# A hybrid decoder layer in split fp32: the first hidden group of both FFNs becomes six plain up steps, with the activation blocks combined beside them

## The chip, the cores and the metric

The kernel runs on one NeuronCore of a Trainium2 chip. The time is device microseconds of one launch, the median of three runs. The profile is one execution, recorded by the hardware profiler; all its times count from the start of its span.

## The reference, cut to what matters

One layer of a decoder over 544 tokens (512 of a prompt, 32 of samples), held as columns: activations are 128 partitions x 8 tiles x 544 tokens, the tokens in two halves of 272. Four sub-layers follow one another; the change touches the first and the third.

```python
def swiglu(h, w_in, w_out):
    gu = h @ w_in
    g, u = jnp.split(gu, 2, axis=-1)
    return (jax.nn.silu(g) * u) @ w_out

x = x + 0.5 * rmsnorm(swiglu(rmsnorm(x, f1_pre), f1_in, f1_out), f1_post)     # f1
...                                                                            # mixer
x = x + 0.5 * rmsnorm(swiglu(rmsnorm(x, f2_pre), f2_in, f2_out), f2_post)     # f2
...                                                                            # gated embedding
```

D_MODEL is 1024 (KD = 8 tiles of 128), D_FF is 2816 (F_TILES = 22 tiles of 128).

## The kernel before, in words

**Split fp32.** Every dense product is done as three fp32r products: each operand is split into a high part (a ScalarE copy, `w_hi`, `a_hi`, `h_hi`) and the rest (a VectorE subtraction, `w_lo`, `a_lo`, `h_lo`), and TensorE runs hi x hi, hi x lo, lo x hi. So each weight tile goes HBM -> `raw` (two slots, queue of SyncE) -> ScalarE -> VectorE -> TensorE. The load of weight w waits until weight w-2 is split.

**Groups.** An FFN runs over the 22 hidden tiles in groups, `GROUPS = (8, 8, 6)`: the up steps of a group (`f1_up0`), then its down products (`f1_down0`), then the next group. An up step makes one hidden tile: gate and up product, norm factor (`out_of`, L1911 and L1912), silu on ScalarE, product, split (`h_hi`, `h_lo`). Down products are 8 (KD) per group; each reads all hidden tiles of the group, 6 matmuls of 272 columns per tile, so 48 with 8 hidden tiles and 36 with 6. Partial sums of the groups are added in `y`.

**Plain and mixed steps.** The first `PLAIN` = 4 up steps of an FFN are plain (`dense`, L570): 8 k-tiles x gate and up x 3 x 2 halves = 96 matmuls. The other 18 are mixed (`up_mixed`, L765): a Strassen-like scheme over 2 x 2 blocks (k-tiles 0 to 3 and 4 to 7, by token halves) with 7 block products instead of 8, so 84 matmuls. It needs combined activation blocks: the normed values (`block_values`, L1990), two differences (L2001, L2003), two sums (L2009, L2012), and the split of seven blocks (`block_high` L1400, `block_low` L1996). Combined weights are made in `mix_front`. In the kernel before all this block work is put among the plain steps, and the last blocks lie in `a_hi`, `a_lo`, which the last plain step must have read (`a_gone`).

**Order.** Each engine has one instruction stream written by hand. On ScalarE and VectorE a weight split stands in it between the other work; an engine whose next instruction waits holds all behind it. The plain steps of f2 begin in halves (`edge_first`, `edge_second`): steps 0 to 2 of f2 are computed before the norm factor of the second half is known.

**End of an FFN.** The last group's down products 4 to 7 stand beside the first weight splits of the next stage, in the order that `edge_splits` gives:

```python
return {4: [(last, 5), (last, 6)], 5: [(last, 7), after[0]], 6: [after[1]], 7: after[2:]}
```

The splits at key 4 wait until down product 3 is done. The squares of each finished `y` tile are summed on GpSimd (L2623), and TensorE sums them over partitions (L604) in the middle of the last down product.

Of the kernel before, what the change touches and what calls it, by code (L numbers as in the profile page):

```python
# [13 lines left out]
F32 = mybir.dt.float32  # L14
# [6 lines left out]
P = 128  # L21
# [16 lines left out]
GROUPS = (8, 8, 6)  # L38
G_FIRST = (0, 8, 16)
G_MAX = max(GROUPS)  # L40
PLAIN = 4
# [74 lines left out]
def build(nc, a, o):  # L116
# [13 lines left out]
    with ctx:  # L130
# [122 lines left out]
        b_part = {11: y[:, 0:4, 0, :], 12: y[:, 0:4, 1, :], 21: y[:, 4:8, 0, :], 22: y[:, 4:8, 1, :]}  # L253
# [60 lines left out]
        def before(m):  # L314
# [31 lines left out]
        sum_quad = {0: (T0["f1_up0"] + 1) % 2, 1: (T0["f1_down2"] + KD - 1) % 2, 2: T0["in"] % 2,  # L346
                    3: T0["f2_up0"] % 2, 4: T0["f2_up0"] % 2, 5: (T0["f2_down2"] + KD - 1) % 2, 6: T0["gate"] % 2,
                    7: T0["end"] % 2}
        EDGES = {0: "in", 1: "f2_up0", 2: "gate"}
        LAST = {0: ("f1_down2", KD - 1), 1: ("out", 3), 2: ("f2_down2", KD - 1), 3: ("gate", 3)}  # L350
# [11 lines left out]
        for name in ("f1_down2", "f2_down2"):  # L362
            for n in range(3):
                PLACED[W0[name] + 5 + n] = tuple(t_[:, 1280 * n:1280 * (n + 1)] for t_ in a_flat)
# [3 lines left out]
        PLACED[W0["f2_up0"] + 2] = tuple(t_[:, 4 * T:4 * T + SLOT] for t_ in h_flat)  # L368
# [178 lines left out]
        def _(pe):  # L547
# [202 lines left out]
            def up_mixed(name, first, n):  # L750
# [34 lines left out]
                if first:  # L785
                    body(Step(first), 7 * (f == "f2"))
                    first += 1
                steps(pe, first, n, body)

            def ffn(name, b, first):  # L790
                up_mixed(f"{name}_up0", PLAIN, GROUPS[0])
                product(f"{name}_down0", KD, 1, GROUPS[0], H, h_tiles(first))
                up_mixed(f"{name}_up1", 0, GROUPS[1])
                product(f"{name}_down1", KD, 1, GROUPS[1], H, h_tiles(first + G_FIRST[1]))
                up_mixed(f"{name}_up2", 0, GROUPS[2])
                product(f"{name}_down2", KD, 1, GROUPS[2], H, h_tiles(first + G_FIRST[2]), loop=5, end=KD - 1)
                edge_last(b, H, GROUPS[2], 1)
# [423 lines left out]
            edge_second(1)  # L1221
            plain_end("f2")
# [12 lines left out]
        def _(act):  # L1235
# [161 lines left out]
            def block_high(f, n):  # L1397

                act.wait_ge(*((sig["b_made"], 8 * f + 8) if n < 2 else (sig["t_made"], 4 * f + 4)))
                fn(B_PAIR[n][0], B_RAW[n], ACT.Copy).then_inc(sig["t_hi"], 1)  # L1400

            def plain_end(name):


                f, up0, st, first = int(name == "f2"), f"{name}_up0", Step(PLAIN - 1), Step(PLAIN)
                act.wait_ge(sig["psum_full"], ticket(st, up0)[0])
                mix_front(up0, first)
# [3 lines left out]
                mix_begin(up0, first)  # L1411
                block_high(f, 6)
                snap(up0, first, 0)
                up_gate(up0, st)
                mix_high(up0, first, 1)
                up_high(up0, st)

            def up_mixed(name, first, n):


                def body(st, last=False, begun=False):
                    if not begun:
                        snap(name, st, 0)
# [16 lines left out]
                if first:  # L1440
                    body(Step(first), begun=True)
                    first += 1
                else:
                    mix_high(name, Step(0), 1)
                steps(act, first, n - 1, body)
                body(Step(n - 1), last=True)

            def down0(st, t, quad, use):
# [15 lines left out]
            def ffn(name, b, after):  # L1464

                j = 2 * b + 1
                up_mixed(f"{name}_up0", PLAIN, GROUPS[0])
                stage(f"{name}_down0", KD, down0, follow=f"{name}_up1")
                up_mixed(f"{name}_up1", 0, GROUPS[1])
                stage(f"{name}_down1", KD, lambda st, t, quad, use: None, follow=f"{name}_up2")  # L1470
                up_mixed(f"{name}_up2", 0, GROUPS[2])
                nc.scalar.preload_act_table_set("natural_log_exp_and_others")
                last = f"{name}_down2"
# [32 lines left out]
            stage("f1_up0", GROUPS[0], up("f1_up0"), first=1, end=2)  # L1506
            for n in range(2):
                block_high(0, n)
            stage("f1_up0", GROUPS[0], up("f1_up0"), first=2, end=3)
            block_high(0, 2)  # L1510
            plain_end("f1")
# [227 lines left out]
            norm(4, 1)  # L1739
            split_edge("f2_up0", 3, T0["f2_up0"] + 2)  # L1740
            nc.scalar.preload_act_table(ACT.Silu)
            for c in range(3):
                up("f2_up0")(Step(c), *ticket(Step(c), "f2_up0"))
                for n in ((), (0, 1), (2,))[c]:
                    block_high(1, n)
# [9 lines left out]
            def between(half, k):  # L1755
                if half == 0 and k in (1, 3):
                    e_tiles(k // 2)
                if half == 0 and k == 4:
                    split_edge("gate", 1, T0["f2_down2"] + KD)
                    e_tiles(2)  # L1760
                    e_tiles(3)
# [30 lines left out]
        def _(dve):  # L1792
# [158 lines left out]
            def up_mixed(name, first, n):  # L1951
# [26 lines left out]
                if first:  # L1978
                    body(Step(first))
# [833 lines left out]
```

## Time and profile before

| | |
|---|---|
| median of 3 runs (1239.47 to 1240.24) | 1239.5 us |
| the profiled execution, own time | 1242.34 us |
| its span | 1240.6 us |
| TensorE matmul busy | 1167.4 us (94%) |
| VectorE / ScalarE / GpSimd busy | 801.5 / 565.5 / 98.7 us |
| mean granted TensorE clock | 0.974 |

How to read it: matmuls follow one another closer than a single one lasts (290 ns on average, every 126 ns), so the pace is read from a stretch with its count. TensorE is busy nearly throughout, and its idle stretches are few; which work ends each of them is what counts.

### The profile page before, as it was taken

To read this page: it belongs to the slowest core of one execution; us is meant where nothing else is said; L and a number is where in the kernel's file an instruction comes from. 1 tells how busy PE (TensorE), PEld (TensorE's weight loads), DVE (VectorE), ACT (ScalarE), POOL (GpSimd) and SP (SyncE) were. 2 spreads that over 40 slices of the span, in tenths; PEclk is the share of its full clock that TensorE was granted. 3 is DMA by queue.
4 is the path that set the end of the run, shared out by engine and by line. 5 is a ranking of instruction groups with operands and counts; after the bars stand their busy time and mean duration, and the time that the engine had idled before them with its cause. 6 is when DMAs were issued, how large, how long until landed. Compare 5 with 4: busy or idle time off the path is not lost.

```text
span 1240.6 us, 22901 instructions
## 1 busy us (share of the span) xinstructions
PE 1167.4 (94%) x9150; PEld 1125.3 (91%) x9150; DVE 801.5 (65%) x1103; ACT 565.5 (46%) x776; POOL 98.7 (8%) x139
## 2 busy tenths in 40 slices
PE   7789999999998799999998999879999999999895
PEld 7789999999998789999877699879999999999894
DVE  5796278736854756555378747697268835864666
ACT  5364245523543432311389745355245522553544
POOL 1500000000002002112040010000000000002002
PEclk9899999999999799999998999989999999999997
DMA  5222332224213122113055251122243223314202
GB/s 209 69 68 69 102 121 92 73 88 132 84 52 124 35 69 85 61 63 107 1 167 193 69 170 35 35 72 66 85 136 101 68 86 118 102 39 134 99 1 73
DMA packets 45420, 110.26 MB, mean 89 GB/s; under 512 B 5474, under 2 KB 11634, under 8 KB 45218
## 3 DMA queue, kind: packets, MB, share of 16 engines
q1 hardware_dynamic: 43538, 103.13, 25.4%
q0 software_dynamic: 1232, 5.01, 1.2%
q8 instruction: 52, 0.85, 0.3%
q10 hardware_dynamic: 576, 1.08, 0.2%
q14 instruction: 22, 0.18, 0.0%
HBM read 103.57 MB, written 5.64 MB: 88 GB/s over the span
## 4 chain that ended last, share of the span: by engine, by line
PE 82%; DVE 9%; ACT 5%; issue 2%; DMA 1%; SPq 0%; POOL 0%; DVEq 0%; ACTq 0%
PE PS L570 34%; PE PS L765 29%; PE PS L583 9%; PE PS L880 1%; PE PS L1056 1%; DVE w_lo L1800 1%; PE PS L735 1%; ACT w_hi L1243 1%; PE PS L604 1%; DVE y L1990 1%; PE PS L907 1%; DVE a_lo L1996 1%; DMA raw<-in_ple_w_up 0%; PE PS L937 0%; PE PS L981 0%
## 5 line engine op out<-in xcount | busy, mean ns | idle before, releaser
L1800 DVE TENSOR_TENSOR w_lo<-raw,w_hi 128x1024 fp32r<-128x1024 f32 (+2 forms) x74 | 104.1, 1407 | 111.1 <-ACT w_hi L1243 111.1
L765 PE MATMUL PS<-a_hi,w_hi 128*128 128x272 f32 x576 | 167.0, 290 | 3.4 <-issue 3.4
L765 PE MATMUL PS<-a_lo,w_hi 128*128 128x272 f32 x576 | 167.7, 291 | 0.0
L765 PE MATMUL PS<-a_hi,w_lo 128*128 128x272 f32 x576 | 166.9, 290 | 0.0
L1243 ACT ACTIVATE w_hi<-raw 128x1024 fp32r<-128x1024 f32 (+2 forms) x75 | 88.9, 1185 | 143.1 <-PE PS L570 120.5
L570 PE MATMUL PS<-h_hi,w_hi 128*128 128x272 f32 x632 | 130.9, 288 | 2.0 <-DVE w_lo L1800 2.0
L570 PE MATMUL PS<-a_hi,w_hi 128*128 128x272 f32 x528 | 115.4, 301 | 18.4 <-DVE w_lo L2099 7.1
L570 PE MATMUL PS<-h_hi,w_lo 128*128 128x272 f32 x632 | 130.9, 289 | 0.0
L570 PE MATMUL PS<-h_lo,w_hi 128*128 128x272 f32 x632 | 130.4, 288 | 0.0
L765 PEld LDWEIGHTS PS<-a_hi,w_hi 128*128 128x128 f32 x576 | 109.3, 190 | 4.0 <-issue 3.8
L570 PE MATMUL PS<-a_lo,w_hi 128*128 128x272 f32 x528 | 112.2, 295 | 0.0
L570 PE MATMUL PS<-a_hi,w_lo 128*128 128x272 f32 x528 | 111.8, 294 | 0.0
L765 PE MATMUL PS<-b_tail,w_hi 128*128 128x272 f32 x576 | 110.6, 290 | 0.0
L765 PEld LDWEIGHTS PS<-a_hi,w_lo 128*128 128x128 f32 x576 | 109.2, 190 | 0.0
L765 PEld LDWEIGHTS PS<-a_lo,w_hi 128*128 128x128 f32 x576 | 108.9, 189 | 0.0
L570 PEld LDWEIGHTS PS<-a_hi,w_hi 128*128 128x128 f32 x528 | 86.1, 196 | 22.9 <-issue 13.4
L570 PEld LDWEIGHTS PS<-h_hi,w_hi 128*128 128x128 f32 x632 | 99.4, 188 | 2.4 <-issue 2.4
L570 PEld LDWEIGHTS PS<-h_lo,w_hi 128*128 128x128 f32 x632 | 99.4, 189 | 0.0
L570 PEld LDWEIGHTS PS<-h_hi,w_lo 128*128 128x128 f32 x632 | 98.7, 189 | 0.0
L765 PEld LDWEIGHTS PS<-b_tail,w_hi 128*128 128x128 f32 x576 | 90.8, 189 | 0.0
L570 PEld LDWEIGHTS PS<-a_lo,w_hi 128*128 128x128 f32 x528 | 86.3, 196 | 0.0
L570 PEld LDWEIGHTS PS<-a_hi,w_lo 128*128 128x128 f32 x528 | 85.6, 195 | 0.0
(468 smaller groups left out, 2636.6 us busy)
## 6 DMA issues: line engine op xcount, KB each, us to landing
raw<-in_f_in SPq DMA_DIRECT2D x86, 512.0 KB, 4.3
raw<-in_f_out SPq DMA_DIRECT2D x64, 256.0 KB, 2.8
raw<-in_w_rest SPq DMA_DIRECT2D x40, 256.0 KB, 2.9
raw<-in_f_out SPq DMA_DIRECT2D x32, 192.0 KB, 2.4
raw<-in_w_out SPq DMA_DIRECT2D x8, 512.0 KB, 4.4
raw<-in_ple_w_gate SPq DMA_DIRECT2D x8, 512.0 KB, 4.5
x<-in_x SPq DMA_DIRECT2D x8, 272.0 KB, 6.8
out<-x SPq DMA_DIRECT2D x8, 272.0 KB, 2.2
```

The costliest lines, as they stand in the source:

```text
L570: last = mm(PS[0:width, 4 * quad + 2 * c + half, 0:HALF], wt[:, cols], act[:, k, half * HALF:(half + 1) * HALF], start=(k == 0 and n == 0) ...
L583: last = mm(PS[0:width, 4 * quad + 2 * c + half, 0:HALF], wt[:, cols], act[:, k, tok], start=(k == 0 and n == 0), stop=(k == n_k - 1 and n ...
L604: last = mm(PS[:, 4 * quad + 2 + half, 0:HALF], ones[:], squares[:, tok], start=(k < summed), stop=(k == KD - 1))
L735: last = mm(PS[:, 4 * (t % 2) + 2 * c + half, 0:HALF], wt[:, slot, col:col + P], act[:, k, half * HALF:(half + 1) * HALF], start=(k == 0 a ...
L765: last = mm(PS[:, 4 * quad + bank, 0:HALF], w_[:, k * P:(k + 1) * P], a_[:, k, :], start=(start and k == 0 and i == 0), stop=(stop and k = ...
L880: last = mm(PS[:, 2 + hh, tok], k_[r, tok], q_[r, tok], start=True, stop=True)
L907: last = mm(PS[:, 7, n * 256:n * 256 + 256], kl_batch[:, 2 * part + n, :], gv_new[:, p * 256:(p + 1) * 256], start=True, stop=True)
L1056: last = mm(out, mask, src, start=start and i == 0, stop=stop and i == 1)
L1243: fn(pair[0][:, 0:width], raw[:, slot, 0:width], ACT.Copy).then_inc(sig["split_hi"], 1)
L1800: v.tensor_tensor(pair[1][:, 0:width], raw[:, slot, 0:width], pair[0][:, 0:width].bitcast(F32), ALU.subtract).then_inc(sig["split_lo"], 1)
L1990: v.scalar_tensor_tensor(flat(y[:, k]), flat(x[:, k]), vec[:, c:c + 1], flat(rstd[:, 0]), ALU.mult, ALU.mult).then_inc(sig["b_made"], 1)
L1996: v.tensor_tensor(B_PAIR[n][1], B_RAW[n], B_PAIR[n][0].bitcast(F32), ALU.subtract).then_inc(sig["t_lo"], 1)
```

## The change

- `GROUPS` is (6, 8, 8), and `PLAIN` is the first group: all six up steps of it are plain, its down products (36 matmuls each) come next, and only then the 16 mixed steps.
- The raw blocks of the second token half are written into the slots of hidden tiles 6 and 7, which the first group does not use. `block_values` makes half tiles (16 instructions of 272 columns instead of 8 of 544), some at a time; differences and sums are single instructions between the parts of the plain steps.
- `plain_end` splits the weights of the first two down products, and the last four blocks beside them.

```diff
-GROUPS = (8, 8, 6)
-G_FIRST = (0, 8, 16)
+GROUPS = (6, 8, 8)
+G_FIRST = (0, 6, 14)
-PLAIN = 4
+ENDS = len(GROUPS) - 1
+PLAIN = GROUPS[0]
...
-        b_part = {11: y[:, 0:4, 0, :], 12: y[:, 0:4, 1, :], 21: y[:, 4:8, 0, :], 22: y[:, 4:8, 1, :]}
+        h_end = [scratch(hold_h[:], (n * G_MAX - 2) * T, [P, 4, HALF]) for n in (1, 2)]
+        b_part = {11: y[:, 0:4, 0, :], 12: h_end[0], 21: y[:, 4:8, 0, :], 22: h_end[1]}
...
             def plain_end(name):        # ScalarE
-                act.wait_ge(sig["psum_full"], ticket(st, up0)[0])
-                mix_front(up0, first)
+                split(st, up0, ticket(st, up0)[0])
                 for n in range(3, 6):
                     act.wait_ge(sig["a_gone"], 3 * f + n - 2)
                     block_high(f, n)
-                mix_begin(up0, first)
+                split(Step(0), down0, ticket(Step(0), down0)[0])
+                up_gate(up0, st)
                 block_high(f, 6)
...
-            def block_values(f):
-                for k in range(KD):
+            def block_values(f, half, first, end):
+                for k in range(first, end):
                     c = VEC[f"f{f + 1}_pre"] + k
-                    v.scalar_tensor_tensor(flat(y[:, k]), flat(x[:, k]), vec[:, c:c + 1], flat(rstd[:, 0]), ALU.mult,
+                    v.scalar_tensor_tensor(b_part[10 * (k // 4 + 1) + half + 1][:, k % 4, :], x[:, k, half, :],
+                                           vec[:, c:c + 1], rstd[:, 0, half, :], ALU.mult,
                                            ALU.mult).then_inc(sig["b_made"], 1)
...
             def plain_end(name, j):     # VectorE
+                split(st, up0)
+                block_low(f, 3)
+                block_low(f, 4)
                 out_of(up0, j, st, t, quad, use)
+                split(Step(0), f"{name}_down0")
+                product_of(up0, st, quad, use)
+                block_low(f, 5)
+                up_low(up0, st)
                 block_low(f, 6)
...
-            up("f1_up0", 0)(Step(0), *ticket(Step(0), "f1_up0"))
-            block_values(0)
-            stage("f1_up0", GROUPS[0], up("f1_up0", 0), first=1, end=2)
+            out_of("f1_up0", 0, st, t, quad, use)
+            block_values(0, 0, 0, 1)
+            product_of("f1_up0", st, quad, use)
+            block_values(0, 0, 1, 3)
+            up_low("f1_up0", st)
+            block_values(0, 0, 3, 4)
+            st = Step(1)
+            split(st, "f1_up0")
+            block_values(0, 0, 4, 8)
+            block_values(0, 1, 0, 2)
...
```

**VectorE at the start of f1.** The rows follow the sum of squares; `work<-PS,rstd` is `out_of`, `w_lo<-raw,w_hi 128x2048` the split of the weights of plain step 2. Before:

```order
L1911 TENSOR_TENSOR work<-PS,rstd 128x544
L1912 TENSOR_TENSOR work<-PS,rstd 128x544
L1902 TENSOR_TENSOR work<-work 128x544
L1917 TENSOR_TENSOR h_lo<-work,h_hi 128x544
L1990 SCALAR_TENSOR_TENSOR y<-x,vec,rstd 128x544 x8
L1800 TENSOR_TENSOR w_lo<-raw,w_hi 128x2048
```

VectorE at the same place in the changed kernel:

```order
L1913 TENSOR_TENSOR work<-PS,rstd 128x544
L1914 TENSOR_TENSOR work<-PS,rstd 128x544
L1988 SCALAR_TENSOR_TENSOR y<-x,vec,rstd 128x272
L2020 TENSOR_TENSOR work<-work 128x544
L1988 SCALAR_TENSOR_TENSOR y<-x,vec,rstd 128x272 x2
L1919 TENSOR_TENSOR h_lo<-work,h_hi 128x544
L1988 SCALAR_TENSOR_TENSOR y<-x,vec,rstd 128x272
L1804 TENSOR_TENSOR w_lo<-raw,w_hi 128x2048
L1988 SCALAR_TENSOR_TENSOR y<-x,vec,rstd 128x272 x4
L1988 SCALAR_TENSOR_TENSOR hold_h<-x,vec,rstd 128x272 x2
```

Four half tiles of values stand ahead of the split now instead of eight whole ones.

**VectorE in f2, from the weights of step 3 to those of step 4, in the changed kernel** (`b_extra`, `b_tail` are split blocks, `y<-y,hold_h` and `hold_h<-hold_h` differences, `extra<-` and `y<-extra,y` sums):

```order
L1804 TENSOR_TENSOR w_lo<-raw,w_hi 128x2048
L2020 TENSOR_TENSOR work<-work 128x544
...
L2002 TENSOR_TENSOR y<-y,hold_h 128x4x272
L1988 SCALAR_TENSOR_TENSOR hold_h<-x,vec,rstd 128x272 x4
L1913 TENSOR_TENSOR work<-PS,rstd 128x544
L1914 TENSOR_TENSOR work<-PS,rstd 128x544
L1995 TENSOR_TENSOR b_tail<-y,b_tail 128x1088
L2020 TENSOR_TENSOR work<-work 128x544
L2005 TENSOR_TENSOR hold_h<-hold_h 128x1088
L1919 TENSOR_TENSOR h_lo<-work,h_hi 128x544
L2012 SCALAR_TENSOR_TENSOR extra<-y,hold_h 128x1088
L2015 SCALAR_TENSOR_TENSOR y<-extra,y 128x4x272
L1804 TENSOR_TENSOR w_lo<-raw,w_hi 128x2048
```

On ScalarE the block copy that needs the last sum stands ahead of the same weights' high part:

```order
L1402 ACTIVATE b_tail<-y 128x1088
L1245 ACTIVATE w_hi<-raw 128x2048
```

In the kernel before there was no plain weight to split after the sums: step 3 was the last plain step, and the mixed weights came next.

**ScalarE beside down products 4 to 7 of the last group of f1.** Before:

```order
L1460 ACTIVATE sq<-y 128x544
L1243 ACTIVATE a_hi<-raw 128x768 x2
L1460 ACTIVATE sq<-y 128x544
L1243 ACTIVATE a_hi<-raw 128x768
L1243 ACTIVATE w_hi<-raw 128x2048
L1460 ACTIVATE sq<-y 128x544
```

The same place in the changed kernel:

```order
L1456 ACTIVATE sq<-y 128x544
L1245 ACTIVATE a_hi<-raw 128x1024 x2
L1456 ACTIVATE sq<-y 128x544
L1245 ACTIVATE a_hi<-raw 128x1024
L1245 ACTIVATE w_hi<-raw 128x2048
L1456 ACTIVATE sq<-y 128x544
```

The order is the same; the down weights are 1024 columns instead of 768, since the last group has 8 hidden tiles.

## Rows read from the trace of the kernel before

**Rows 1.** The page, busy time, share of the span and instructions of each engine

```profile
PE 1167.4 (94%) x9150; PEld 1125.3 (91%) x9150; DVE 801.5 (65%) x1103; ACT 565.5 (46%) x776; POOL 98.7 (8%) x139
```

**Rows 2.** TensorE timeline, plain to mixed steps: start, us, instruction, idle before it

```profile
42.20 0.82 PE L570 MATMUL PS<-a_hi,w_hi 128*128 128x272 f32 x2 [6.42 <-DVE w_lo L1800]
...
69.20 0.52 PE L765 MATMUL PS<-b_extra,w_hi 128*128 128x272 f32 x2 [0.94 <-DVE w_lo L1939]
...
79.66 0.36 PE L765 MATMUL PS<-a_hi,w_hi 128*128 128x272 f32 x1 [2.43 <-issue]
...
800.22 0.70 PE L570 MATMUL PS<-a_hi,w_hi 128*128 128x272 f32 x2 [3.73 <-DVE work L1912]
...
820.57 0.82 PE L765 MATMUL PS<-b_extra,w_hi 128*128 128x272 f32 x2 [6.54 <-DVE w_lo L1939]
```

**Rows 3.** TensorE by stretch: us, PE busy (matmuls), clock, DMA share, GB/s

```profile
42.20:56.00 13.80, 13.80 (x96) 0.86 0.33 102
79.66:84.00 4.34, 4.34 (x22) 0.61 0.02 4
```

**Rows 4.** The chain that ended last: start us, us, what

```profile
116.21 48.11 PE PS L570 x384
164.32 84.74 PE PS L765 x672
...
366.22 13.81 PE PS L570 x108
...
407.34 1.29 PE PS L604 x2
...
1116.44 13.81 PE PS L570 x108
...
1154.08 1.19 PE PS L604 x4
```

**Rows 5.** VectorE timeline, start of f1

```profile
30.16 0.72 DVE L1911 TENSOR_TENSOR work<-PS,rstd 128x544 f32<-128x544 f32 x1 [3.12 <-ACT rstd L1276]
...
34.30 5.65 DVE L1990 SCALAR_TENSOR_TENSOR y<-x,vec,rstd 128x544 f32<-128x544 f32 x8
39.86 2.29 DVE L1800 TENSOR_TENSOR w_lo<-raw,w_hi 128x2048 fp32r<-128x2048 f32 x1
...
48.49 1.30 DVE L2001 TENSOR_TENSOR y<-y 128x1088 f32<-128x1088 f32 x1
```

**Rows 6.** ScalarE timeline, start of f1

```profile
33.53 1.90 ACT L1243 ACTIVATE w_hi<-raw 128x2048 fp32r<-128x2048 f32 x1
...
45.90 1.11 ACT L1400 ACTIVATE b_tail<-y 128x1088 fp32r<-128x1088 f32 x1
```

**Rows 7.** VectorE timeline, edge into f2

```profile
771.86 0.50 DVE L1832 SCALAR_TENSOR_TENSOR a_lo<-x,vec,a_hi 128x272 fp32r<-128x272 f32 x1
772.27 0.50 DVE L1820 SCALAR_TENSOR_TENSOR work<-y,vec,rstd 128x272 f32<-128x272 f32 x1
...
787.06 0.79 DVE L2492 TENSOR_TENSOR work<-PS,rstd 128x272 f32<-128x272 f32 x2 [4.90 <-ACT rstd L1276]
```

**Rows 8.** TensorE timeline, last down products of f1

```profile
366.22 0.51 PE L570 MATMUL PS<-h_hi,w_hi 128*128 128x272 f32 x2 [0.99 <-DVE w_lo L1800]
...
395.76 0.36 PE L583 MATMUL PS<-h_hi,a_hi 128*128 128x272 f32 x1 [2.22 <-DVE y L2034]
...
403.22 0.73 PE L604 MATMUL PS<-sum_sq,ones 128*128 128x272 f32 x2 [3.09 <-POOL sum_sq L2623]
```

**Rows 9.** VectorE and GpSimd timelines, weight splits of down products

```profile
111.28 1.23 DVE L1800 TENSOR_TENSOR w_lo<-raw,w_hi 128x1024 fp32r<-128x1024 f32 x1 [2.12 <-ACT w_hi L1243]
...
368.17 0.96 DVE L1800 TENSOR_TENSOR w_lo<-raw,w_hi 128x768 fp32r<-128x768 f32 x1 [1.46 <-ACT w_hi L1243]
...
372.52 1.36 POOL L2623 TENSOR_TENSOR sum_sq<-sum_sq,sq 128x544 f32<-128x544 f32 x1 [4.42 <-ACT sq L1460]
...
373.21 1.49 DVE L1800 TENSOR_TENSOR w_lo<-raw,w_hi 128x768 fp32r<-128x768 f32 x1 [1.46 <-ACT w_hi L1243]
```

More of the change, by code:

```diff
@@ L783, in body @@
                     part(7, 6, 0, False, True).then_inc(sig["psum_full"], 1)
[L785 to L788, printed above, removed]
+                if begin:
+                    body(Step(0), 7 * (f == "f2"))
+                steps(pe, int(begin), n, body)
             def ffn(name, b, first):
[L791 to L797, printed above, removed]
+                product(f"{name}_down0", KD, 1, PLAIN, H, h_tiles(first))
+                for n in range(1, ENDS + 1):
+                    up_mixed(f"{name}_up{n}", GROUPS[n], n == 1)
+                    last = dict(loop=5, end=KD - 1) if n == ENDS else {}
+                    product(f"{name}_down{n}", KD, 1, GROUPS[n], H, h_tiles(first + G_FIRST[n]), **last)
+                edge_last(b, H, GROUPS[ENDS], 1)
             pe.wait_ge(sig["masks_made"], 1)
@@ L1221, in _ @@
             edge_second(1)
+            product("f2_up0", PLAIN - 1, 2, KD, A, first=3)
             plain_end("f2")
@@ L1466, in ffn @@
                 j = 2 * b + 1
[L1467 to L1471, printed above, removed]
+                stage(f"{name}_down0", KD, down_first, first=1, follow=f"{name}_up1")
+                for n in range(1, ENDS):
+                    up_mixed(f"{name}_up{n}", GROUPS[n])
+                    stage(f"{name}_down{n}", KD, lambda st, t, quad, use: None, follow=f"{name}_up{n + 1}")
+                up_mixed(f"{name}_up{ENDS}", GROUPS[ENDS])
                 nc.scalar.preload_act_table_set("natural_log_exp_and_others")
-                last = f"{name}_down2"
+                last = f"{name}_down{ENDS}"
                 stage(last, KD, down1(j), end=1)
@@ L1505, in _ @@
             up("f1_up0")(Step(0), *ticket(Step(0), "f1_up0"))
[L1506 to L1509, printed above, removed]
+            st = Step(1)
+            split(st, "f1_up0", ticket(st, "f1_up0")[0])
+            block_high(0, 0)
+            up("f1_up0")(st, *ticket(st, "f1_up0"))
+            st = Step(2)
+            split(st, "f1_up0", ticket(st, "f1_up0")[0])
+            block_high(0, 1)
+            up("f1_up0")(st, *ticket(st, "f1_up0"))
             block_high(0, 2)
+            stage("f1_up0", PLAIN, up("f1_up0"), first=3, end=PLAIN - 1)
             plain_end("f1")
@@ L1739, in _ @@
             norm(4, 1)
+            nc.scalar.preload_act_table(ACT.Silu)
+            up("f2_up0")(Step(0), *ticket(Step(0), "f2_up0"))
             split_edge("f2_up0", 3, T0["f2_up0"] + 2)
[L1741 to L1745, printed above, removed]
+            block_high(1, 0)
+            up("f2_up0")(Step(1), *ticket(Step(1), "f2_up0"))
+            block_high(1, 1)
+            up("f2_up0")(Step(2), *ticket(Step(2), "f2_up0"))
+            block_high(1, 2)
+            stage("f2_up0", PLAIN, up("f2_up0"), first=3, end=PLAIN - 1)
             plain_end("f2")
@@ L2005, in block_sums @@
[L2005 to L2012 removed]
+                dve.wait_ge(sig["b_made"], 16 * f + 12 + 4 * n)
```

172 lines of the change are left out of this document (93 added, 79 removed).

## The prediction, before the run

> **What bounds the kernel now.** I read the page first: TensorE is busy 94% of the span [rows 1], so a change pays only by fewer or faster matmuls, or by less of the remaining idle time. The chain of waits says how fast: eight down products of eight hidden tiles are 384 matmuls in 48.11 us, 0.1253 us each, and eight mixed steps are 672 in 84.74 us, 0.1261 each [rows 4]. So a plain step costs 96 x 0.1253 = 12.03 us, a mixed one 10.59, a down product 6.01 us over eight hidden tiles and 4.51 over six. Then I looked in TensorE's timeline for each start with idle time before it. In f1 they are 6.42, 0.94 and 2.43 us, in f2 3.73 and 6.54 [rows 2], all among the first steps. The releaser is mostly VectorE: a weight's low part that stands behind block work in its stream. After two of the long ones the clock is at 1.2 instead of 2.4 GHz for some us: 96 matmuls took 13.80 us (1.8 too many), 22 took 4.34 (1.6 too many) [rows 3]. The last place is the end of an FFN: 0.99, 2.22 and 3.09 us of idle time among the last down products [rows 8].
>
> **The added matmuls.** Two more steps per FFN are plain: 2 x (96 - 84) = 24 matmuls, 24 x 0.1253 = 3.0 us each FFN, +6.0 in all. That is on the path and certain. What comes back must be read from the waits. I do it by placing TensorE in time, from the last point that the change leaves alone to the start of the fifth down product of the last group (I call it s4), which is three products of 4.51 behind the second one: 366.22 + 13.5 = 379.75 in f1, 1116.44 + 13.5 = 1129.97 in f2 [rows 4].
>
> **Start of f1.** TensorE ends step 1 at 42.20 - 6.42 = 35.78 [rows 2]. VectorE begins at 30.16 [rows 5]. Before, all values (5.65 us) stood ahead of the weights of step 2, whose low part began at 39.86. Now four half tiles do. Their price is not in the trace; the nearest row is an operation of the same kind, two tensors and a column scale on 272 columns, 0.50 us, the next one starting 0.41 later [rows 7]. The bounds: 5.65/16 = 0.35 if only columns counted, 0.50 if nothing overlapped. I take 0.41. Four of them fit ahead of 35.4, where ScalarE has made the high part (33.53 + 1.90) [rows 6], so the split runs 35.45 to 37.74 (2.29) [rows 5], and step 2 starts at 37.8: a wait of 2.0 instead of 6.42.
> The Trainium skill (VectorE: DVE Perf Modes, on the TRN2 errata) speaks against the cut into halves: SBUF operations pay a fixed cost per instruction, so small tiles pay it more often. By its cycle table a half tile would be an estimated 0.34 us; the eight in f2's chain below would take 0.6 us less than by my 0.41, and the sum would be 1214.4. The row decides here.
> Does the clock fall after a wait of 2.0? It did after 2.43 and 6.42; after 0.94 the next matmuls kept their pace. I take no fall, and +1.8 as the bound; about 0.6 of that would only eat the next wait.
> From 37.65 VectorE has: six half values 2.5, `out_of` 1.3, a block's low part 1.2, product 0.65, two values 0.8, `h_lo` 0.65, a difference 1.2: the weights of step 3 are split by 48.2, needed at 37.8 + 12.03 = 49.8. Free. Then four values and a low part to 51.0, `out_of` 1.3, difference 1.2, product 0.65 and sum 1.2 with the waits between them, `h_lo` 0.65, the second sum 1.3 (a 1088-column operation lasts 1.30 [rows 5]): 57.2. ScalarE copies that sum, 1.1 us, and only then makes the high part of step 4's weights, 1.9 [rows 6], VectorE the low part, 2.3: 62.45, where step 3 ends at 61.85. Wait 0.6. Steps 4 and 5 end at 62.45 + 24.05 = 86.5; no split stands behind more than an `out_of` there.
> The first down product reads hidden tile 5 last, 30 matmuls in, at 90.3. That tile needs `out_of` 1.4, the split of the second down weights 0.9, product 0.65, one block's low part 1.25, `h_lo` 0.7: 91.4. Wait 1.1.
>
> **Rest of f1.** Eight down products of 4.51, eight mixed steps, eight down products of 6.01, eight mixed steps, four down products of 6.01: 86.5 + 1.1 + 36.1 + 84.7 + 48.1 + 84.7 + 24.05 = 365.3. Before: 379.75. So s4 comes 14.5 us earlier. Of it, +3.0 are matmuls, -10 the waits and slow clock at the start. The other -7 are this: eight products of the first group are 1.5 us shorter each (-12.0), while ahead of s4 only four of the last group are longer (+6.0), and the 0.99 us there goes: the second weights come 5.2 us after the first product's start, which now lasts 6.01.
> In the first group the short products must leave room for the next mixed weights. Those are two ScalarE and VectorE splits of 3.3 us together behind the start of the last down product, 4.51 long: hidden, with 1 us to spare, and +1 per FFN if not.
>
> **Start of f2.** Steps 0 to 2 are unchanged; step 2 ends at 800.22 - 3.73 = 796.5 [rows 2]. VectorE used to wait 4.90 us until 787.06 [rows 7]; eight half values (3.3) lie in it now. After 787.85 come three half values, product and `h_lo` of step 0, `out_of` of step 1 by 792.6: bank free, so the 3.73 goes. Weights of step 3 are split by 794.8, before 796.5. Then, behind them: product, value, `h_lo` to 796.9; low part, difference, four values to 800.9; `out_of`, low part, product, difference, `h_lo`, two sums to 808.45; then ScalarE's copy and high part and VectorE's low part, 1.1 + 1.9 + 2.3: 813.75. Step 3 ends at 808.5. So **a new wait of 5.2 us** stands before step 4 of f2, with the clock down behind it (+1.8, as after 6.42). Step 5 ends at 813.75 + 13.85 + 12.05 = 839.7. The same 1.1 as in f1, then 36.1 + 84.7 + 48.1 + 84.7 + 24.05: s4 at 1118.4, before 1129.97: 11.5 us earlier.
>
> **Behind s4.** Here TensorE is not the bound. The chain runs from the splits that wait for s4 over the loads of the next stage's weights, their splits and the eviction of down product 6 that stands behind them, to the sums at 407.34 and 1154.08 [rows 4]. It hangs on s4, not on how long the products last: TensorE itself would reach its half-way sum at s4 + 4 x 6.01 - 1.1 = 22.95, against 27.6 and 24.1 now. So the longer products 4 to 7 fill the waits of 2.22 and 3.09 and cost nothing. What lengthens the chain is the width of the splits ahead of the first load: 1.23 against 0.96 us for 1024 and 768 columns [rows 9], on both engines, and the next split after it; where GpSimd adds at the same time VectorE's took 1.49 instead of 0.96, so I add the same 0.53 to the wide one. Together +0.75 per FFN, between 0.3 and 1.5.
>
> **Sum.** -14.5 - 11.5 + 1.5 = -24.5 us. The profiled execution took 1242.34 against a span of 1240.6; the 1.7 around it do not change, and I take the difference from the median of the runs, 2.8 below that execution: 1239.5 - 24.5 = 1215.0.
>
> **Rivals.**
> *The end of an FFN stretches with its products* (12%). If the chain behind s4 hangs on later products after all (a load that waits for the split of the seventh weight, an eviction in the queue), products 4 to 7 cost their 6 us in each FFN: 1227. For it: each split at a key of `edge_splits` waits for its own product. Against it: TensorE waits 5.3 us there now.
> *The start gains less* (10%). Low parts and `h_lo` miss their slots, and step 5 and the first down product wait like step 4 of f2: two more waits of 3 to 4 us with some slow clock per FFN, or the whole start gain lost (10 and 7.5 us): 1223 to 1232.
> *The end gains more* (8%). The in-order chain in f2 is 2 us shorter than I count and the clock stays up: 1210.
> *Slower* (3%). Each of plain steps 2 to 5 gets its weights as late as step 2 did before, 6.4 us and 1.8 of slow clock: eight times 8.2 against the 9.6 that I count for all waits of both starts, +56: 1271. It decides from 4.3 us on average per step, where the 24.5 are used up. Only one place, f2's step 4, reaches that by my count.
> *The clock.* The Trainium skill (TensorE: Matmul & The Clock Gate, "What's actually happening") says that the check of activity runs freely and does not start anew with the kernel, so that the same wait can be followed by a fall in one run and not in another. By that page step 4 of f2 might keep its pace, 1213.2, and step 2 of f1 might not, 1216.2. The rows show both kinds only for different waits.
>
> **The numbers.** Likeliest 67%: 1215.0, with 1211 to 1219 from the bounds (half values at 0.35 or 0.50: 1 us either way in f2; the clock -1.8 or +1.2; behind s4 -0.9 or +1.5). The range reaches to the second and third case: 1209 to 1225. A measurement of this kernel tells 0.2%, 2.5 us, from no change. Faster 0.94, within 0.2% 0.02, slower 0.04 (1% of it for what I have not seen).
>
> **What would show it.** In the changed kernel's profile: step 2 of f1 starts near 37.8; idle time of 0 to 1 us before step 4 of f1 and about 5 before step 4 of f2, released by VectorE's weight split; about 1 us inside the first down product of both; the last group of f1 reaches s4 near 365; the waits of 0.99 and 2.22 are gone and that of 3.09 is under 1.5; the half-way sum comes 28 us after s4 in f1. It is wrong if f2's wait is over 8 us, if the first mixed step waits for weights, or if the stretch behind s4 is longer than before by more than 2 us.

## The result, and the profile after

| | before | after |
|---|---|---|
| median of the runs on the same chip | 1239.87 us (1239.47 to 1242.61, 4 runs) | 1217.64 us (1217.07 to 1218.09, 4 runs) |
| ratio, 95% interval | | 0.9818 [0.9804, 0.9833] |
| span of the profiled execution | 1240.6 us | 1216.0 us |
| mean granted TensorE clock | 0.974 | 0.985 |

The change takes 22.2 us off; forecast were 24.5, a time of 1215.0. The two spans differ by 24.6, but 2.4 of that belong to the execution of before that was profiled: from the block of 108 matmuls at the end of f1 to the block of 264 ahead of f2, where no line was changed, it took 290.7 us, while the changed kernel and those of experiments 1 and 2 took 288.2 to 288.3. I leave these 2.4 out below.

The page of after, busy time by engine (before: [rows 1]):

```profile
PE 1163.2 (96%) x9198; PEld 1122.2 (92%) x9198; DVE 784.5 (65%) x1095; ACT 554.2 (46%) x756; POOL 97.5 (8%) x139
```

48 matmuls more, and yet TensorE is busy 4.2 us less: the slow clock of [rows 3] is gone from f1 (some of the 4.2 are slow clock in the 2.4 above). Of TensorE's timeline after, the starts that stand behind idle time (before: [rows 2] and [rows 8]):

```profile
38.02 0.52 PE L573 MATMUL PS<-a_hi,w_hi 128*128 128x272 f32 x2 [2.04 <-DVE w_lo L1804]
62.82 0.52 PE L573 MATMUL PS<-a_hi,w_hi 128*128 128x272 f32 x2 [0.43 <-DVE w_lo L1804]
91.97 0.52 PE L573 MATMUL PS<-h_hi,w_hi 128*128 128x272 f32 x2 [1.03 <-DVE h_lo L1919]
...
385.09 0.36 PE L586 MATMUL PS<-h_hi,a_hi 128*128 128x272 f32 x1 [0.69 <-DVE y L2040]
392.56 0.72 PE L607 MATMUL PS<-sum_sq,ones 128*128 128x272 f32 x2 [2.33 <-POOL sum_sq L2660]
396.61 1.28 PE L607 MATMUL PS<-sq,ones 128*128 128x272 f32 x2 [3.33 <-ACT sq L1300]
...
799.86 0.82 PE L573 MATMUL PS<-a_hi,w_hi 128*128 128x272 f32 x2 [5.34 <-DVE w_lo L1804]
831.17 0.52 PE L573 MATMUL PS<-h_hi,w_hi 128*128 128x272 f32 x2 [1.03 <-DVE h_lo L1919]
```

Step 2 of f1 waits 2.04 instead of 6.42, the mixed steps no longer wait for weights, and the 3.73 of f2 is gone, and f2 has its new wait of 5.34 before step 4. At the end of f1 the 0.99 is gone and the 2.22 has become 0.69. The chain that ended last, after (before: [rows 4]):

```profile
124.48 84.76 PE PS L768 x672
209.25 48.10 PE PS L573 x384
...
342.09 24.30 PE PS L573 x192
...
372.00 7.99 DMA raw<-in_w_in
380.07 1.93 ACT w_hi L1245
...
396.61 1.29 PE PS L607 x2
401.79 4.86 PE PS L586 x24
406.65 0.92 PE PS L607 x4
407.56 13.57 PE PS L586 x108
...
799.86 26.54 PE PS L573 x192
...
1081.29 42.34 PE PS L573 x336
...
1135.39 10.55 PE PS L738 x84
```

The last group now reaches s4 at 342.09 + 4 x 6.01 = 366.1 in f1 (379.75 before) and at 1105.3 in f2. VectorE behind step 2 of f2's plain steps, the place of the new wait (columns: start, us, work, idle before it):

```profile
791.93 1.28 DVE L2012 SCALAR_TENSOR_TENSOR extra<-y,hold_h 128x1088 f32<-128x1088 f32 x1
793.25 1.29 DVE L2015 SCALAR_TENSOR_TENSOR y<-extra,y 128x1088 f32<-128x1088 f32 x1
797.52 2.29 DVE L1804 TENSOR_TENSOR w_lo<-raw,w_hi 128x2048 fp32r<-128x2048 f32 x1 [2.98 <-ACT w_hi L1245]
```

The split stands behind both sums and stands still for 2.98 us more, since ScalarE copies the second sum and only then makes the high part.

### The profile page after: what moved, and what is told of

Read it like the earlier page. It is cut to its first block, busy times and chain, and to the rows that moved or that the text cites. A ratio compares the mean times of both kernels' runs of the same rounds, so it can differ in the third digit from the quotient of the medians.

```text
span 1216.0 us, 23032 instructions
## 1 busy us (share of the span) xinstructions
PE 1163.2 (96%) x9198; PEld 1122.2 (92%) x9198; DVE 784.5 (65%) x1095; ACT 554.2 (46%) x756; POOL 97.5 (8%) x139
## 4 chain that ended last, share of the span: by engine, by line
PE 85%; DVE 7%; ACT 4%; issue 2%; DMA 1%; SPq 0%; POOL 0%; DVEq 0%; ACTq 0%
PE PS L573 38%; PE PS L768 28%; PE PS L586 10%; PE PS L881 1%; DVE w_lo L1804 1%; PE PS L738 1%; ACT w_hi L1245 1%; PE PS L1057 1%; PE PS L607 1%; PE PS L908 1%; DMA raw<-in_w_in 1%; PE PS L938 0%; DVE hold_h L1988 0%; DVE work L2020 0%; PE PS L982 0%
## 5 line engine op out<-in xcount | busy, mean ns | idle before, releaser
L1804 DVE TENSOR_TENSOR w_lo<-raw,w_hi 128x1024 fp32r<-128x1024 f32 (+2 forms) x78 | 111.1, 1424 | 102.6 <-ACT w_hi L1245 102.6
L1245 ACT ACTIVATE w_hi<-raw 128x1024 fp32r<-128x1024 f32 (+2 forms) x79 | 95.2, 1205 | 143.9 <-PE PS L573 122.8
L573 PE MATMUL PS<-a_hi,w_hi 128*128 128x272 f32 x656 | 140.8, 297 | 16.1 <-DVE w_lo L1804 7.8
L768 PE MATMUL PS<-a_lo,w_hi 128*128 128x272 f32 x512 | 148.7, 290 | 0.0
L768 PE MATMUL PS<-a_hi,w_lo 128*128 128x272 f32 x512 | 147.6, 288 | 0.0
L768 PE MATMUL PS<-a_hi,w_hi 128*128 128x272 f32 x512 | 147.4, 288 | 0.0
L573 PE MATMUL PS<-a_lo,w_hi 128*128 128x272 f32 x656 | 138.1, 292 | 0.0
L573 PE MATMUL PS<-a_hi,w_lo 128*128 128x272 f32 x656 | 137.6, 291 | 0.0
L573 PEld LDWEIGHTS PS<-a_hi,w_hi 128*128 128x128 f32 x656 | 105.1, 193 | 20.7 <-issue 9.6
L573 PEld LDWEIGHTS PS<-a_lo,w_hi 128*128 128x128 f32 x656 | 105.6, 193 | 0.0
L573 PEld LDWEIGHTS PS<-a_hi,w_lo 128*128 128x128 f32 x656 | 105.2, 193 | 0.0
L768 PE MATMUL PS<-b_tail,w_hi 128*128 128x272 f32 x512 | 98.0, 289 | 0.0
L768 PEld LDWEIGHTS PS<-a_hi,w_hi 128*128 128x128 f32 x512 | 96.6, 189 | 0.0
L768 PEld LDWEIGHTS PS<-a_hi,w_lo 128*128 128x128 f32 x512 | 96.4, 188 | 0.0
L768 PEld LDWEIGHTS PS<-a_lo,w_hi 128*128 128x128 f32 x512 | 96.0, 188 | 0.0
L768 PEld LDWEIGHTS PS<-b_tail,w_hi 128*128 128x128 f32 x512 | 80.3, 188 | 0.0
```

Source lines behind the costliest of these rows:

```text
L573: last = mm(PS[0:width, 4 * quad + 2 * c + half, 0:HALF], wt[:, cols], act[:, k, half * HALF:(half + 1) * HALF], start=(k == 0 and n == 0) ...
L768: last = mm(PS[:, 4 * quad + bank, 0:HALF], w_[:, k * P:(k + 1) * P], a_[:, k, :], start=(start and k == 0 and i == 0), stop=(stop and k = ...
L1245: fn(pair[0][:, 0:width], raw[:, slot, 0:width], ACT.Copy).then_inc(sig["split_hi"], 1)
L1804: v.tensor_tensor(pair[1][:, 0:width], raw[:, slot, 0:width], pair[0][:, 0:width].bitcast(F32), ALU.subtract).then_inc(sig["split_lo"], 1)
```

## The experiments

All ratios are against the kernel before, run on the same chip. Experiments 1, 2, 4 and 5 shared one chip, 6 to 9 one, 3 and 10 one.

**1. The group sizes alone.**

```diff
-GROUPS = (8, 8, 6)          # before
-G_FIRST = (0, 8, 16)
+GROUPS = (6, 8, 8)          # PLAIN stays 4
+G_FIRST = (0, 6, 14)
```

> The kernel before with only the group sizes changed, 6, 8 and 8 instead of 8, 8 and 6 (the first group is four plain and two mixed steps); no plain step is added and the block work stands as before. Theory of the prediction: TensorE does the same matmuls and reaches the fifth down product of the last group 6.0 us earlier (eight shorter products ahead of it, four longer) plus the 0.99 us wait, and the stretch behind it is longer by 0.75 us: 1.5 + 1.5 less, about -6.2 per FFN, -12.5 in all, 1227. With the size of the stretch as the trace after the change has it (2.9 us longer in f1, 1.2 in f2): 14.0 - 4.1, about -9.9, 1229.9. Rival, the end of an FFN stretches with its products: the sum of products is the same, only the waits of 0.99 go, -2, 1237.5. The waits at the start of both FFNs (6.42, 2.43, 3.73, 6.54) stay as they are under all of them.

Measured: 1226.83 us, ratio 0.9895 [0.9881, 0.9910], so -13.0 by the ratio (-11.1 to -14.8). The starts behind idle time at the beginning of f1 and f2:

```profile
42.04 0.82 PE L570 MATMUL PS<-a_hi,w_hi 128*128 128x272 f32 x2 [6.43 <-DVE w_lo L1800]
...
811.52 0.82 PE L765 MATMUL PS<-b_extra,w_hi 128*128 128x272 f32 x2 [6.55 <-DVE w_lo L1939]
```

The waits at the start stand as before. More than half of the whole gain comes from nothing but the order of the group sizes, in the size that the prediction gave it (-12.5); the -9.9 worked out with the longer stretches of after lies outside the interval. The rival that the end stretches with its products is out.

**2. Two more plain steps alone.**

```diff
-PLAIN = 4                   # before; GROUPS stays (8, 8, 6)
+PLAIN = 6
+            product("f2_up0", PLAIN - 1, 2, KD, A, first=3)                   # TensorE
+            stage("f1_up0", GROUPS[0], up("f1_up0", 0), first=3, end=PLAIN - 1)
```

(the last line so in both FFNs, on ScalarE and VectorE)

> The kernel before with only two more plain steps in each FFN (six plain and two mixed in a first group of eight), block work and group sizes as before. 24 more matmuls per FFN cost 6.0 us in all. Theory backlog (the waits in the first mixed step, 0.94 and 2.43 with 1.6 of slow clock in f1 and 6.54 in f2, are VectorE's backlog from the block work, and two more plain steps let it catch up): those go, 6.0 - 5.0 - 6.5 = -5.5, 1234; the waits before step 2 (6.42 and 3.73) stay. Theory placement (those waits come from the block parts that stand between the last plain step and the first mixed one, and go with them to the new place): +6.0, 1245.5, with waits of the same length before the seventh step.

Measured: 1238.76 us, ratio 0.9995 [0.9986, 1.0003]: no difference, and neither theory. TensorE's starts behind idle time among the steps of f1 and f2:

```profile
42.41 0.82 PE L570 MATMUL PS<-a_hi,w_hi 128*128 128x272 f32 x2 [6.44 <-DVE w_lo L1803]
...
100.96 0.36 PE L765 MATMUL PS<-a_hi,w_hi 128*128 128x272 f32 x1 [0.55 <-issue]
...
796.47 0.49 PE L570 MATMUL PS<-a_hi,w_hi 128*128 128x272 f32 x2 [3.73 <-DVE work L1915]
815.41 0.82 PE L570 MATMUL PS<-a_hi,w_hi 128*128 128x272 f32 x2 [5.14 <-DVE w_lo L1803]
```

Backlog is right in f1: the 0.94 and 2.43 are gone, 0.55 is left. In f2 the 6.54 did not stay at the first mixed step and did not go either: it became 5.14 before step 4, which is now plain. So a wait for the split behind the block sums is there with whole values and the old order too; the half values did not make it. With the group sizes this explains 13.6 us if the two add up, which no run tests; the remaining 8.6 of the 22.2 (worked out, not run by itself) then belong to the block work beside the plain steps.

**3. The interleaved half values of f1 undone.**

```diff
-            block_values(0, 0, 3, 4)       # after, VectorE, f1
+            block_values(0, 0, 3, 8)
+            block_values(0, 1, 0, 8)
             st = Step(1)
             split(st, "f1_up0")
-            block_values(0, 0, 4, 8)
-            block_values(0, 1, 0, 2)
...
-            block_values(0, 1, 2, 4)
...
-            block_values(0, 1, 4, 8)
```

> The changed kernel with one part of the change undone, in f1 only: all sixteen half block values stand ahead of the split of step 2's weights on VectorE, as the eight whole ones did before, instead of four. Theory of the prediction: twelve more operations of 0.41 us start to start push the split back by 4.9 us: the wait before step 2 is 6.9 instead of 2.04, longer than the 6.42 of before since sixteen halves take 6.6 and eight whole ones took 5.65, and the clock falls behind it (1.8): +6.7 at most, 1223 to 1224, less what the later steps catch up (the 0.4 before step 4). Rival, the half values are cheap where no ScalarE work is between them (0.35): a wait of 6.2. Rival, the place does not matter because the wait moves from step 4's weights to step 2's: +2 or less.

Measured: 1223.22 us, ratio 0.9864 [0.9841, 0.9887], that is 5.7 to 6.7 us above the changed kernel by the ratios (0.9818 and, once more on another chip, 0.9810). VectorE and TensorE:

```profile
36.25 3.39 DVE L1988 SCALAR_TENSOR_TENSOR hold_h<-x,vec,rstd 128x272 f32<-128x272 f32 x8
39.57 2.29 DVE L1804 TENSOR_TENSOR w_lo<-raw,w_hi 128x2048 fp32r<-128x2048 f32 x1
```

```profile
41.91 0.82 PE L573 MATMUL PS<-a_hi,w_hi 128*128 128x272 f32 x2 [6.25 <-DVE w_lo L1804]
```

The wait is back, at 6.25 instead of the 6.9 forecast, and the clock was down behind it (81 matmuls in the next 12.1 us instead of 96). The eight half values took 3.39, so 0.42 each, and the rival's 0.35 is out, although its 6.2 comes close; I had counted all twelve as added time, but in the changed kernel the split waits 0.62 for ScalarE (35.67, behind four values), which the values now fill. Stated rightly the sum is 2.04 + 4.9 - 0.6 = 6.3.

**4. The split of step 4's weights ahead of the block sums.**

```diff
             up_low("f1_up0", st)           # after, VectorE; f2 alike
+            st = Step(3)
+            split(st, "f1_up0")
+            block_sum(0, 0)
             block_sum(0, 1)
...
+            st = Step(3)                   # ScalarE
+            split(st, "f1_up0", ticket(st, "f1_up0")[0])
             block_high(0, 2)
```

(the first sum stood two lines higher in f1)

> The changed kernel with one order changed on ScalarE and VectorE in both FFNs: the split of the weights of step 4 stands ahead of the two block sums (VectorE) and ahead of the copy of the third block part (ScalarE). Theory of the prediction: the wait of 5.34 us before step 4 of f2 is that split standing behind the sums and the copy; it goes, with about 1.8 us of slow clock behind it, and the 0.43 us in f1: -7.5, 1210.1. Rival, the delay only moves: the sums and the block parts behind them come 2.3 us later (the length of the split) and the waits turn up before step 5 or in the first down product: -3 to -5, 1213 to 1215. Second rival, the split waits for its load or for a buffer that step 2 frees: then the wait keeps 3 us or more.

Measured: 1207.43 us, ratio 0.9744 [0.9731, 0.9757], 8 to 9 us below the changed kernel by the ratios. The profile is of an execution that took 1211.71 and in which the clock fell behind step 2 of f1 (granted 0.52 from 38.5 to 42), so its waits are read here and not its span. TensorE in f2, and VectorE there:

```profile
793.80 0.52 PE L573 MATMUL PS<-a_hi,w_hi 128*128 128x272 f32 x2 [0.53 <-DVE w_lo L1810]
822.97 0.52 PE L573 MATMUL PS<-h_hi,w_hi 128*128 128x272 f32 x2 [1.03 <-DVE h_lo L1925]
```

```profile
791.46 2.29 DVE L1810 TENSOR_TENSOR w_lo<-raw,w_hi 128x2048 fp32r<-128x2048 f32 x1 [0.70 <-ACT w_hi L1245]
793.67 1.28 DVE L2018 SCALAR_TENSOR_TENSOR extra<-y,hold_h 128x1088 f32<-128x1088 f32 x1
```

5.34 became 0.53, the 0.43 of f1 is gone, and 192 matmuls behind it took 24.4 us instead of 26.54. Nothing behind it got later: 1.03 in the first down product as before. Both rivals are out; the wait was the order in two streams.

**5. The last group's sixth down weights split one product earlier.** They are (last, 5). The seventh and eighth stay beside the same products as before; but since `raw` has two slots, the load of the eighth, which waits for the split of the sixth, starts one product earlier, and the next stage's first load no longer has it just ahead.

```diff
-            return {4: [(last, 5), (last, 6)], 5: [(last, 7), after[0]], 6: [after[1]], 7: after[2:]}
+            return {3: [(last, 4), (last, 5)], 4: [(last, 6)], 5: [(last, 7), after[0]], 6: [after[1]], 7: after[2:]}
...
-                stage(last, KD, down1, first=1, end=4)       # ScalarE and VectorE
-                for c in range(4, KD):
+                stage(last, KD, down1, first=1, end=3)
+                for c in range(3, KD):
```

> The changed kernel with the weights of the sixth down product of the last group (index 5) split one product earlier, behind the fourth instead of the fifth, together with index 4, and the next ones one earlier too. So the load of the last down weights, which waits for a buffer, starts one product (6.0 us) earlier and isn't beside the load of the next stage's first weights any more. Theory: what made the stretch behind the fifth down product longer than predicted in f1 (30.5 us instead of 28.3) is that the next stage's load took 7.99 us with the other load beside it, against 5.28 before: it comes back to 5.3 to 6, the stretch falls to 28, -2.5 in f1 and 0 to -2 in f2: 1213 to 1215. Rival, the load is as long by itself or another link of the chain ends last (VectorE's splits, the sum of squares): no change, 1217.6 +- 1.

Measured: 1211.44 us, ratio 0.9777 [0.9763, 0.9791], 4 to 5 us below the changed kernel by the ratios. Its chain at the end of f1:

```profile
342.29 30.31 PE PS L573 x240
...
376.96 4.63 DMA raw<-in_w_in
...
402.93 13.58 PE PS L586 x108
```

The load in this chain is another than in the chain of after. The next stage's first weights and its second are 1 MB each, loaded in two parts of 512 KB. In after the chain runs over the load of the first, here over that of the second, which waits until the eighth down weights are split. ScalarE here:

```profile
375.31 1.92 ACT L1245 ACTIVATE w_hi<-raw 128x2048 fp32r<-128x2048 f32 x1 [0.32 <-DMA raw<-in_w_in]
...
381.67 1.92 ACT L1245 ACTIVATE w_hi<-raw 128x2048 fp32r<-128x2048 f32 x1 [0.79 <-DMA raw<-in_w_in]
```

The load of the first, like for like with the 7.99 of after, was issued at 370.98 and took 4.25 us; its split starts 9.0 us behind s4 (366.3) instead of 14.0 (380.07 - 366.1). Of these 5.0 us 3.7 are the shorter load, the rest its earlier start. The stretch from s4 to the block of 108 matmuls is 36.6 us, against 41.4 after, and only one of the two wide splits stands behind a load in this chain now. In f2 the stretch from s4 to L738's 84 matmuls fell from 30.1 to 27.7. The two stretches together are 7.2 us shorter, the ratios say 4 to 5: in this execution the unchanged code between the FFNs took 290.7 us again instead of 288.3.

The edit took away two neighbours of the load at once. In after the second weights' load was issued at 376.40 and ran beside the first's until 379.99; here it was issued at 376.59, behind the first's end. So the experiment shows that the load is shorter without both, and not which of them had made it long.

**6. The changed kernel once more.** No edit.

> The changed kernel itself once more, beside the others on one chip. Expected ratio 0.982 again. What it tells: whether the 7.99 us of the next stage's first load in f1 repeats. In early_split4, with the same loads beside it, it took 6.62. Theory overlap (the load of the last down weights runs beside it): 6.3 to 8.3 again. Rival, scatter of that load from one execution to the next: 5.0 to 6.0 this time.

Measured: 1216.99 us, ratio 0.9810 [0.9787, 0.9832]. Of its chain:

```profile
342.93 24.29 PE PS L573 x192
...
372.84 7.58 DMA raw<-in_w_in
...
408.16 13.57 PE PS L586 x108
```

The long load repeats: 7.99 and 7.58 here, 6.62 in experiment 4, 8.29 in experiment 3. Experiment 1, whose last group has the same width, had 6.9. The theory of overlap holds, with a scatter of 1.7 us in it. With the narrower last weights beside it (two loads of 192 instead of 256 KB) it was shorter, in the chain of the kernel before:

```profile
385.37 5.28 DMA raw<-in_w_in
...
419.15 13.57 PE PS L583 x108
```

and 5.09 in experiment 2. With the other load landed ahead of it, the same load took 4.0 to 4.3 us in experiments 5 and 7 to 9, and 5.46 in experiment 10.

**7. Experiments 4 and 5 together.** The edit is both diffs above.

> The two orders of early_split4 and early_w5 together in the changed kernel. Against the 22.2 us that the change gave, early_split4 gave 9.8 more and early_w5 5.8 more. Theory, two separate places (the start of an FFN and the end of its last group): they add, 22.2 + 9.8 + 5.8 = 37.8 below the kernel before, 1201.7. Rival, they share something (a longer load in one profile, a clock level): only the larger one and a part of the other, 1204 to 1207.

Measured: 1205.59 us (1203.55 to 1206.42), ratio 0.9719 [0.9695, 0.9742]: 34.8 below the kernel before. The gains of 4 and 5 over the changed kernel would add up to a ratio of 0.9744 + 0.9777 - 0.9818 = 0.9703, which lies in the interval, so a sum is not contradicted; but the 1201.7 worked out from medians was not reached, the time lies in the range of the rival (1204 to 1207), and the interval does not exclude that a part is shared. The trace has both effects: 0.53 at 789.78 in f2, and in f1 a load of the next stage's first weights of 4.0 us.

**8. The low part behind the hidden tile.** In 7, `plain_end` on VectorE:

```diff
-                block_low(f, 5)
                 up_low(up0, st)
+                block_low(f, 5)
                 block_low(f, 6)
```

> both_early, with VectorE's low part of the third block difference (1.28 us) moved behind the low part of the last plain step's hidden tile. Theory of the prediction: the 1.03 us inside the first down product of each FFN is that low part standing ahead of it in VectorE's stream; the wait goes, -1.0 per FFN, -2.0 against both_early. Rival, the hidden tile's low part waits for ScalarE's high part (which stands behind one more block part there): then only 0.2 to 0.3 us of it go, under -0.6 in all.

Measured: 1204.88 us, ratio 0.9718 [0.9696, 0.9741]: not told apart from 7. The wait went from 1.03 to 0.65 in both FFNs:

```profile
38.02 0.58 PE L573 MATMUL PS<-a_hi,w_hi 128*128 128x272 f32 x2 [2.04 <-DVE w_lo L1810]
92.43 0.52 PE L573 MATMUL PS<-h_hi,w_hi 128*128 128x272 f32 x2 [0.65 <-DVE h_lo L1925]
```

The block part was 0.4 us of the 1.03; for the rest the rival was right: the hidden tile's low part now stands still for 0.72 us until ScalarE has made the high part. The first row is told of below.

**9. The split of step 2's weights one place earlier, in f1.** In 8:

```diff
-            up("f1_up0")(Step(0), *ticket(Step(0), "f1_up0"))    # ScalarE
+            up_gate("f1_up0", Step(0))
             st = Step(1)
             split(st, "f1_up0", ticket(st, "f1_up0")[0])
+            up_high("f1_up0", Step(0))
...
-            block_values(0, 0, 1, 3)                            # VectorE
-            up_low("f1_up0", st)
-            block_values(0, 0, 3, 4)
+            block_values(0, 0, 1, 2)
             st = Step(1)
             split(st, "f1_up0")
-            block_values(0, 0, 4, 8)
+            up_low("f1_up0", Step(0))
+            block_values(0, 0, 2, 8)
```

> later_low5, with the split of the weights of step 2 of f1 one place earlier on both engines: on ScalarE ahead of the high part of the first hidden tile, on VectorE ahead of its low part and of two more half values. ScalarE stood still for 0.86 us there and its 1.90 us of split then ended at 35.6. Theory: the 2.03 us before step 2 are ScalarE's place for the split; ScalarE starts it at 32.3, VectorE ends it at 36.6 instead of 37.9, and step 2 waits 0.7: -1.3 against later_low5. Rival, the split waits for its load (raw weights) or for step 0's slot: no change.

Measured: 1202.49 us (1200.50 to 1204.98), ratio 0.9699 [0.9675, 0.9724]. TensorE, then VectorE:

```profile
36.12 0.52 PE L573 MATMUL PS<-a_hi,w_hi 128*128 128x272 f32 x2 [0.51 <-DVE w_lo L1811]
```

```profile
33.77 2.29 DVE L1811 TENSOR_TENSOR w_lo<-raw,w_hi 128x2048 fp32r<-128x2048 f32 x1 [0.60 <-ACT w_hi L1245]
```

2.04 became 0.51; the wait was the split's place behind the first hidden tile, as the theory had it. Both engines' orders were changed together; that VectorE's split still waits 0.60 for ScalarE says that the two values ahead of it are not what is late. The median is 2.4 below that of 8, forecast were 1.3, and the intervals of the two ratios overlap.

**10. The hidden tile's high part ahead of the fourth block part.** In 9, `plain_end` on ScalarE:

```diff
-                block_high(f, 6)
                 up_high(up0, st)
+                block_high(f, 6)
```

> early_split2, and in both FFNs ScalarE copies the high part of the last plain step's hidden tile ahead of the fourth block part instead of behind it. later_low5 left 0.65 us of the 1.03 us before the first down product's last tile. Theory: what is left is ScalarE's 1.1 us block copy ahead of the high part; it goes, TensorE starts that tile without a wait in both FFNs, -0.65 each, -1.3 in all against early_split2 (which took 0.9699 of the kernel before): 0.9688. Rival, the high part waits for VectorE's product anyway: the wait stays at 0.5 to 0.65. A clock fall in some executions moves the time by more than this (2 us), so the wait in the trace decides, not the median.

Measured: 1201.67 us (1201.12 to 1204.29), ratio 0.9691 [0.9670, 0.9712]; not told apart from 9 by time, and the wait is 0.65 as before. VectorE's chain to it:

```profile
86.04 0.71 DVE L1921 TENSOR_TENSOR work<-PS,rstd 128x544 f32<-128x544 f32 x1
86.67 0.95 DVE L1811 TENSOR_TENSOR w_lo<-raw,w_hi 128x768 fp32r<-128x768 f32 x1
87.54 0.72 DVE L2027 TENSOR_TENSOR work<-work 128x544 f32<-128x544 f32 x1
88.98 0.73 DVE L1926 TENSOR_TENSOR h_lo<-work,h_hi 128x544 fp32r<-128x544 f32 x1 [0.73 <-ACT h_hi L1365]
```

The rival was right. What is left is the chain `out_of`, weight split, product, high part, low part; the split of the second down weights (0.95) stands in it, and it was not tried to move it. Kernels 7 to 10 beat both the kernel before and the changed one by more than their intervals; 9 and 10 are the fastest, 37 and 38 us below the kernel before by their ratios.

## Why the prediction was right, and where its 2.3 us went

By its own steps:

- **The added matmuls**, +6.0: right. The granted clock apart, the pace is the forecast one: 672 in 84.76, 384 in 48.10.
- **Start of f1**: step 2 at 38.02 (37.8 forecast, and everything in this execution is some 0.2 later), its wait 2.04 (2.0) without a clock fall, 0.43 before step 4 (0.6), 1.03 inside the first down product (1.1). Four half values in 1.73 us, 0.41 from start to start, as taken. The difference to the forecast grows in tenths: 0.2 at step 2, 0.4 at step 4, 0.6 at the last hidden tile, 0.8 at s4, which came at 366.1 instead of 365.3. So -13.6 instead of -14.5.
- **Start of f2**: the 3.73 is gone, 5.34 stands before step 4 (5.2), 1.03 in the down product (1.1). Counted from the block of 264 matmuls ahead of f2 (709.83 before, 695.83 after), s4 came 10.6 us earlier, forecast 11.5. The wait was right; the term for the slow clock was low: 192 matmuls took 26.54, 2.15 more than the 24.39 of the same matmuls in experiment 4, instead of 1.8. It scatters: 25.97 in experiment 5, 26.66 in experiment 6. The Trainium skill (VectorE: DVE Perf Modes, on the TRN2 errata) says that a small SBUF operation pays a fixed cost again. The trace agrees in that: half tiles came 0.41 to 0.42 apart, more than half of the whole tiles' 0.71 (5.65 / 8). My estimate of 0.34 from its table was too low.
- **Behind s4**, the step that failed. The prediction said that the chain there "hangs on s4, not on how long the products last", and that it is lengthened only by "the width of the splits ahead of the first load", +0.75 per FFN. It does hang on s4 (experiment 1), but it also grew by the load itself, which I had left at its old length: 5.28 us before, 7.99 and 7.58 after. The widths, which I had made the whole of it, are seen in the time from s4 to the load's start: 5.6 us before (385.37 - 379.75), 5.9 after (372.00 - 366.1), so +0.3. From s4 to the block of 108 matmuls f1 took 39.4 us before and 41.4 and 41.2 after, so about +1.9 instead of +0.75. (By the half-way sum it is +2.9, 30.5 against 27.6; the 24 matmuls behind it then took 4.86 instead of 5.71 us.) In f2, from s4 to L735's (after: L738's) 84 matmuls, it was 29.6 before, 30.1 and 29.7 after, +0.1 to +0.4. "That of 3.09 is under 1.5" was wrong (2.33), and "the half-way sum comes 28 us after s4" too (30.5): more than 2 us longer than before, the sign that the prediction had named for a wrong step. Experiment 5 shows that the overlap with other loads is the cause: with the last down weights loaded earlier the same load took 4.25 us and the stretch 36.6. Which of the loads beside it counts, the one ahead or the one behind, is not shown.

The sum by these places: -13.6 - 10.6 + 1.9 + 0.3 = -22.0, where -22.2 was measured. The forecast's mechanism was right in every place but one, and the sizes made out the difference: 1.8 at the two starts, 0.7 behind s4. One term was luck, the clock behind step 2 of f1, told of next.

Of the rivals, "the end stretches with its products" (1227) is out by experiment 1, "the start gains less" by the waits above, "slower" too. "The end gains more" did not happen by itself, but 5 and 7 show that it was there to be had. The clock rival is the interesting one. Step 2 of f1 waited 2.02 to 2.09 us in the changed kernel and in experiments 4 to 8. Behind that wait the clock fell in the profiled executions of 4 and 8, and in the other four it did not. TensorE's clock behind it in 7 (both_early) and in 8 (later_low5), each by stretches of us, PE busy (matmuls), clock, DMA share, GB/s:

```profile
38.50:42.00 3.50, 3.50 (x28) 1.00 0.71 222
42.00:46.00 4.00, 4.00 (x34) 1.00 0.18 74
```

```profile
38.50:42.00 3.50, 3.50 (x18) 0.53 0.83 275
42.00:46.00 4.00, 4.00 (x34) 1.00 0.07 28
```

The same wait to 0.01 us, the same work, and in one execution TensorE went on at 2.4 GHz, in the other at 1.2 GHz until about 42, ten matmuls or 1.3 us behind. The Trainium skill (TensorE: Matmul & The Clock Gate, "What's actually happening") says that the check of activity runs freely. These traces agree with that: behind this wait and before this work both were seen. So my "no fall" for a wait of 2.0 us was a guess that came out, not a rule.

## What to carry to other kernels

When a change moves work among engines, a wait of the busy engine can be read off the order in the streams before anything runs: write down for each weight split what stands ahead of it on both engines that make it, and put the split first and the work with slack behind it; that alone gave 8 to 9 us here (experiment 4), and 1.5 us of wait in experiment 9. The size of the pieces at the end of a chain (which group comes last) can be worth more than the work saved inside: 13 of 22 us. And a load on the path keeps its old length in an estimate only if what flies beside it stays the same.

## What the hardware showed beyond that

- A load of 512 KB, the second part of the next stage's first weights, on SyncE's queue in f1: 5.1 and 5.3 us with two loads of 192 KB just ahead of it, 6.6 to 8.3 with two of 256 KB, 4.0 to 4.3 with them landed before (once 5.46). With the second weights' two parts, which follow it, the bytes of the first two cases differ by 5%, the times by 1.3 to 3.2 us. Why so much stays open; the runs only show that it goes when the loads do not overlap.
- A clock fall moves single executions: kernels 7 to 10 have executions at a mean granted clock of 0.989 to 0.990 and others at 0.985 to 0.987, some 2 to 4 us longer. In unchanged code between the FFNs, 48 matmuls of one pass took 7.6 to 7.8 instead of 6.2 us at one place in all twelve profiles (582.23 before, 569.02 after), and at a second place in three of them (before, experiments 5 and 10).
